# When modulation pieces are issued and reduced in the gate layer, an eviction ahead of a split, and attention heads in groups

## The chip, the cores and the metric

The kernel runs on one NeuronCore of a Trainium2 chip. The metric is the device time of one execution in microseconds (us), lower is better. TensorE (PE) multiplies, VectorE (DVE) and ScalarE (ACT) do elementwise work, GpSimd (POOL) helps them, and SyncE (SP) issues nearly all DMAs that bring weights from HBM.

## What is computed

Two transformer parts on one sequence of 256 tokens of width 1024, everything in float32. The first is a block with three kinds of attention and a gated feed-forward layer with a convolution. The second has two layers, each modulated by a condition vector. Cut to what matters here:

```
for layer in range(2):
    shift_m, scale_m, gate_m, shift_f, scale_f, gate_f = ada_mod(c, ada_w[layer], ada_b[layer])
    h = modulate(rms_norm(x, norm_gains[layer, 0]), shift_m, scale_m)
    y = attn_hybrid_mixer(...) if layer % 2 == 0 else retention_mixer(...)
    x = x + gate_m * y
    h = modulate(rms_norm(x, norm_gains[layer, 1]), shift_f, scale_f)
    x = x + gate_f * swiglu(h, w_gate_up[layer], w_down[layer])
return rms_norm(x, final_norm)
```

`ada_mod` is `silu(c) @ w + b` with a matrix of 1024 x 6144 per layer. `attn_hybrid_mixer` has eight "stick" heads (stick-breaking attention) and eight "moba" heads (softmax attention), on projections `qkv` (1024 to 3072), and an output projection (1024 to 1024). `swiglu` is `(silu(gate) * up) @ w_down` with 2816 hidden features.

## The kernel before

**Weights and chunks.** The work is a chain of phases, each a matrix product with its weights cut into chunks: `w_in`, `w_out`, `up`, `down`, `qkv` (12 chunks), `att_o` (4), `gu0` (22, the gate and up weights of layer 0), `dn0` (16, the down weights), `ret_in` (24), `ret_o`, `gu1`, `dn1`. A chunk is 16 tiles of 128x128 (1 MB), or 11 tiles in the down phases (0.7 MB). SP loads chunk n into the ring `raw0` to `raw3` (L582) when the chunk four before has been split. For float32 accuracy each weight is split in two rounded parts: ScalarE writes `w_hi` (L725, `hi(chunk)`), then VectorE `w_lo = raw - w_hi` (L2009, `lo(chunk)`), each in two halves, into two slots. A slot is free when TensorE has finished the chunk two before. TensorE then does three matmuls for each tile (L1330, L1331, L1332: hi x hi, lo x hi, hi x lo), so 48 for a full chunk and 33 for a down chunk. Results go to the PSUM banks `lin[0]` and `lin[1]` in turn; a bank must be evicted (`lin_free`) before the second next chunk starts in it.

**Modulation pieces.** The product with `ada_w` isn't done on TensorE. It comes in 48 pieces of 1 MB; SP loads a piece into one of two slots (L572, `load_ada`), and VectorE reduces it (L2093, two passes, then L2096 adds the bias; `piece`). `load_ada` waits until the piece two before has been reduced (`ada_out`), since it overwrites its slot, and everything that SP issues afterwards stands behind that wait. `ADA_STEPS` says at which step c of a phase a piece stands. Both SP and VectorE walk the phases in that order: SP issues a chunk's weights and then the step's piece; VectorE in step c splits chunk c+1 (`lo`), multiplies (`product`) or evicts, and then reduces the step's piece. The loops are unrolled by four; `steps(eng, n, lead, tail, body)` writes `lead` steps out first and `tail` last, and the pattern must repeat within the loop.

**Attention of layer 0.** The chunks of `qkv` and `att_o` are interleaved with the attention of heads, on TensorE in the table `HOOKS`: `{chunk: {tile number: stages}}` runs stages ahead of that tile. Stages work on pairs of heads: `stick_scores` (L1779, L1781), `stick_sums` (L1791 to L1793), `rotate_heads` (L1801), `moba_scores` (L1838, L1840), `moba_turn` (transposes, L1849), and `stick_values` and `moba_values` (L1813, L1815). These are plain float32 matmuls. The results of the value stages go to two banks in turn; ScalarE rounds them (`round_pair`, L1071), VectorE takes the remainder (`pair_to_split`, L2383, counted by `o_tiles`), and the next but one pair's values wait for that. The first two chunks of `att_o` are done in two parts each (`out_part`), tiles 0 to 3 and 4 to 7. VectorE evicts an `att_o` chunk with L2346 (`out(step)`), which adds it to `x`. Chunks 8 to 11 of `qkv` are wide rows (L1395 to L1398, 512 columns, 0.24 us each).

Of the kernel before, what the change touches and what calls it, by code (L numbers as in the profile page):

```python
# [110 lines left out]
def phase_of(chunk):  # L111
    for ph in ORDER:
        if chunk < ph.chunk0 + ph.n:
# [8 lines left out]
             ("gu0", 22, lambda c: int(4 <= c <= 20 and (c % 2 or c in (4, 18, 20)))), ("dn0", 16, lambda c: int(c % 2 or c in (2, 12)))]  # L122
# [4 lines left out]
def ada_before(name, c):  # L127

    n = 0
    for at, steps_, f in ADA_STEPS:  # L130
        if at == name:
            return n + sum(f(i) for i in range(c))
        n += sum(f(i) for i in range(steps_))


def ada_here(name, c):
    return ADA_AT[name](c) if name in ADA_AT else 0
# [139 lines left out]
def build(nc, dram):  # L277
    ctx = ExitStack()
    with ctx:
# [279 lines left out]
        def _(sp):  # L559
# [25 lines left out]
            def phase(ph):  # L585
                load = weights_of(ph)

                def one(step):
                    load(step)
                    if ph.name == "w_in" and step.j == 1:  # L590
                        sp.dma_start(cond_silu, dram["cond"]).then_inc(cond_in, 16)
                    if ph.name == "w_in" and step.j == 2:
                        sp.dma_start(arena[:, TAB1_AT:TAB1_AT + dram["tab1"].shape[1]], dram["tab1"]).then_inc(tab1_in, 16)
                    for m in range(ada_here(ph.name, step.j)):
                        load_ada(step, lambda c, m=m: ada_before(ph.name, c) + m)

                if ph.name == "qkv":

                    for c in range(ph.n):
                        load(Step(c))  # L600
                        for m in range(ada_here(ph.name, c - 2) if c >= 2 else 0):
                            load_ada(Step(c - 2), lambda c, m=m: ada_before(ph.name, c) + m)
                else:
                    steps(sp, ph.n, *{"gu0": (6, 1), "down": (4, 1), "dn0": (4, 1)}.get(ph.name, (4, 0)), one)
# [96 lines left out]
        def _(act):  # L701
# [252 lines left out]
            ph = PH["up"]  # L954
# [207 lines left out]
            round_pair(0)  # L1162
            hi(ph.chunk0 + 12)
            round_pair(1)
# [3 lines left out]
            qkv_unit(10)  # L1168
            hi(ph.chunk0 + 13)
            qkv_unit(11)  # L1170
            round_pair(3)
# [155 lines left out]
        def _(pe):  # L1327
# [524 lines left out]
            def run(*todo):  # L1852
# [6 lines left out]
                3: {8: run((stick_scores, 0)), 12: run((stick_scores, 1))},  # L1859
                4: {6: run((stick_scores, 2)), 10: run((stick_scores, 3))},  # L1860
                5: {8: run((rotate_heads, 0))},
                6: {6: run((rotate_heads, 1)), 10: run((stick_sums, 0), (stick_sums, 1)), 13: run((stick_sums, 2), (stick_sums, 3))},
# [3 lines left out]
                10: {0: run((moba_turn, 0)), 3: run((stick_values, 0)), 5: run((stick_values, 1)), 6: run((moba_scores, 2))},  # L1866
                11: {0: run((moba_turn, 1)), 2: run((stick_values, 2)), 4: run((moba_scores, 3)), 6: run((stick_values, 3))},
# [31 lines left out]
            out_part(0, range(0, 4), {0: run((moba_turn, 2)), 5: run((moba_values, 0))})  # L1899
            out_part(1, range(0, 4), {0: run((moba_values, 1)), 4: run((moba_turn, 3)), 6: run((moba_values, 2))})  # L1900
# [86 lines left out]
        def _(dve):  # L1987
# [455 lines left out]
            pair_to_split(0)  # L2443
            score_moba(2)
            pair_to_split(1)
            lo(ph.chunk0 + 12)
            weigh_moba(2)
            pair_to_split(2)
            score_moba(3)
            pair_to_split(3)  # L2450
# [11 lines left out]
            for c in range(1, ph.n):  # L2462
                lo(ph.chunk0 + c + 1)
                out(Step(c - 1))
                if c >= 2:
                    z_rest(L0F, ph, c - 2)
# [5 lines left out]
            def swiglu(ph, base, i):  # L2472
# [20 lines left out]
                steps(dve, ph.n, 6 if ph.name == "gu0" else 4, 1, one)  # L2493
# [340 lines left out]
```

## Time and profile before

| | us |
|---|---|
| median of 3 runs (1119.17 to 1120.69) | 1119.7 |
| the profiled execution | 1118.62 |
| its span | 1116.8 |
| TensorE busy | 1068.5 |
| VectorE busy | 792.2 |
| ScalarE busy | 595.3 |

Rows of the timeline give start and duration in us, engine, line, operation, the tile written and the tiles read, shape and count; in brackets stands the idle time of the engine before the row and what ended it. `SPq` rows are DMA issues. The ends of matmuls are modelled, and two matmuls overlap, so the distance between starts is a better measure than the duration.

### The profile page before, as it was taken

Reading aid. Unit: us, or ns where it says so; the run is one execution under the profiler, and the core shown is the slowest. Engines: PE = TensorE matmul, PEld = TensorE weight load, DVE = VectorE, ACT = ScalarE, POOL = GpSimd, SP = SyncE. Lnnn points to the kernel's source line nnn. Section 1 sums busy time; section 2 is a strip of 40 time slices with the busy share of each in tenths; the row PEclk is TensorE's granted clock in tenths of the full one; section 3 lists DMA queues with packets and bytes.
Section 4 is the critical chain, followed back from the end, with each engine's and each line's share of the span. In section 5 each row is a group of like instructions: output and inputs, shape, how many; then the busy total and the mean of one; then the engine's idle time right before and its main releaser. Section 6 shows DMA issues by size and latency. Waiting matters only on the chain.

```text
span 1116.8 us, 21680 instructions
## 1 busy us (share of the span) xinstructions
PE 1068.5 (96%) x8385; PEld 1027.0 (92%) x8385; DVE 792.2 (71%) x1375; ACT 595.3 (53%) x1016; POOL 142.6 (13%) x146
## 2 busy tenths in 40 slices
PE   6988999999899999999999999899999999999998
PEld 5877999999899998789999999897899999999997
DVE  5767659999877887667877778877557757544443
ACT  6586447776344465656544434544365557444442
POOL 0000003343210000013111101210000013111010
PEclk9999989999999899999999999999999999999999
DMA  9621345675698463255674797564434544554450
GB/s 366 216 101 51 146 188 226 253 296 194 251 348 331 161 228 120 79 208 207 255 310 173 307 352 292 221 207 181 136 129 151 189 172 156 202 188 153 156 181 38
DMA packets 34399, 226.66 MB, mean 203 GB/s; under 512 B 3827, under 2 KB 4124, under 8 KB 12444
## 3 DMA queue, kind: packets, MB, share of 16 engines
q1 hardware_dynamic: 33884, 223.11, 53.3%
q0 software_dynamic: 448, 2.63, 0.6%
q8 instruction: 45, 0.74, 0.3%
q14 instruction: 22, 0.18, 0.0%
HBM read 224.66 MB, written 2.63 MB: 204 GB/s over the span
## 4 chain that ended last, share of the span: by engine, by line
PE 74%; DVE 12%; ACT 6%; DMA 4%; issue 2%; POOL 1%; SPq 0%; DVEq 0%; ACTq 0%; POOLq 0%
PE psum L1330 20%; PE psum L1331 19%; PE psum L1332 19%; DVE w_lo L2009 4%; DVE arena L2093 3%; ACT w_hi L725 2%; PE psum L1395 2%; PE psum L1398 2%; PE psum L1397 2%; PE psum L1408 1%; DMA raw<-in_down 1%; DMA raw<-in_dn 1%; PE psum L1427 1%; DMA raw<-in_qkv 1%; DVE arena L2040 1%
## 5 line engine op out<-in xcount | busy, mean ns | idle before, releaser
L2009 DVE TENSOR_TENSOR w_lo<-raw,w_hi 128x1024 fp32r<-128x1024 f32 (+1 forms) x354 | 395.9, 1141 | 214.6 <-ACT w_hi L725 207.2
L725 ACT ACTIVATE w_hi<-raw 128x1024 fp32r<-128x1024 f32 (+1 forms) x354 | 337.7, 971 | 281.4 <-PE psum L1332 188.6
L1330 PE MATMUL psum<-h_hi,w_hi 128*128 128x256 f32 (+1 forms) x1240 | 355.8, 287 | 8.7 <-DVE w_lo L2009 3.1
L1331 PE MATMUL psum<-h_lo,w_hi 128*128 128x256 f32 (+1 forms) x1240 | 349.3, 282 | 0.0
L1332 PE MATMUL psum<-h_hi,w_lo 128*128 128x256 f32 (+1 forms) x1240 | 348.0, 281 | 0.0
L1330 PE MATMUL psum<-hid_hi,w_hi 128*128 128x256 f32 (+1 forms) x1096 | 313.4, 286 | 19.3 <-DVE w_lo L2009 11.6
L1332 PE MATMUL psum<-hid_hi,w_lo 128*128 128x256 f32 (+1 forms) x1096 | 310.4, 283 | 0.0
L1331 PE MATMUL psum<-hid_lo,w_hi 128*128 128x256 f32 (+1 forms) x1096 | 310.4, 283 | 0.0
L1330 PEld LDWEIGHTS psum<-h_hi,w_hi 128*128 128x128 f32 x1240 | 233.6, 188 | 14.1 <-issue 7.8
L1331 PEld LDWEIGHTS psum<-h_lo,w_hi 128*128 128x128 f32 x1240 | 234.6, 189 | 0.7 <-issue 0.7
L1332 PEld LDWEIGHTS psum<-h_hi,w_lo 128*128 128x128 f32 x1240 | 234.7, 189 | 0.0
L1330 PEld LDWEIGHTS psum<-hid_hi,w_hi 128*128 128x128 f32 x1096 | 208.1, 190 | 23.2 <-issue 14.6
L1332 PEld LDWEIGHTS psum<-hid_hi,w_lo 128*128 128x128 f32 x1096 | 208.2, 190 | 0.0
L1331 PEld LDWEIGHTS psum<-hid_lo,w_hi 128*128 128x128 f32 x1096 | 208.1, 190 | 0.0
L2093 DVE CUSTOM_DVE_ANT_0 arena<-arena 128x1024 f32<-128x1024 f32 x96 | 123.8, 1325 | 0.0
L638 POOL TENSOR_TENSOR arena<-arena 128x256 f32<-128x256 f32 x29 | 29.9, 1031 | 482.3 <-ACT arena L1098 331.2
L989 ACT ACTIVATE hid_hi<-arena 128x256 f32 (+1 forms) x60 | 25.1, 418 | 76.8 <-DVE arena L2254 60.7
L658 POOL TENSOR_TENSOR hid_lo<-arena,hid_hi 128x256 f32 (+1 forms) x44 | 35.4, 804 | 182.3 <-ACT hid_hi L989 174.1
L648 POOL TENSOR_TENSOR arena<-arena 128x256 f32<-128x256 f32 x22 | 31.4, 1429 | 85.8 <-ACT arena L978 85.8
L1408 PE MATMUL psum<-busy 128*128 128x256 f32 x221 | 39.2, 337 | 2.5 <-ACT busy L764 2.5
L1408 PEld LDWEIGHTS psum<-busy 128*128 128x128 f32 x221 | 35.2, 238 | 3.0 <-ACT busy L764 2.5
L2244 DVE SCALAR_TENSOR_TENSOR arena<-psum,cols,arena 128x255 f32<-128x255 f32 (+1 forms) x88 | 36.3, 473 | 1.7 <-ACT arena L968 1.0
(245 smaller groups left out, 1021.1 us busy)
## 6 DMA issues: line engine op xcount, KB each, us to landing
arena<-in_ada SPq DMA_DIRECT2D x48, 1024.0 KB, 4.9
raw<-in_gu SPq DMA_DIRECT2D x44, 1024.0 KB, 4.9
raw<-in_ret_in SPq DMA_DIRECT2D x24, 1024.0 KB, 4.8
raw<-in_up SPq DMA_DIRECT2D x22, 1024.0 KB, 7.0
raw<-in_dn SPq DMA_DIRECT2D x32, 704.0 KB, 5.9
raw<-in_qkv SPq DMA_DIRECT2D x12, 1024.0 KB, 7.7
raw<-in_down SPq DMA_DIRECT2D x16, 704.0 KB, 7.4
raw<-in_ret_o SPq DMA_DIRECT2D x8, 1024.0 KB, 4.7
```

Of the source, the lines that this page charges most:

```text
L638: nc.gpsimd.tensor_tensor(acc, acc, sq[:, k * S:(k + 1) * S], ALU.add).then_inc(sq_added, 1)
L648: nc.gpsimd.tensor_tensor(hid, ff["u"][:, 2 * at + S:2 * at + 2 * S], ff["g"][:, at:at + S], ALU.mult)\
L658: nc.gpsimd.tensor_tensor(hid_lo[:, cut], ff["hid"][:, S * (j % 2):S * (j % 2) + S], hid_hi[:, cut].bitcast(F32), ALU.subtract).then_inc(h ...
L725: nc.scalar.activation(w_hi[chunk % SPLIT_SLOTS][:, a:b], raw[chunk % RAW_SLOTS][:, a:b], ACT.Copy)\
L989: nc.scalar.activation(hid_hi[:, bass.ds(step.n(lambda c: (c - lag) * S), S)], ff["hid"][:, S * (j % 2):S * (j % 2) + S], ACT.Copy).then_i ...
L1330: nc.tensor.matmul(out, w[0], hc, start=start, stop=False, skip_group_check=True)
L1331: nc.tensor.matmul(out, w[0], lc, start=False, stop=False, skip_group_check=True)
L1332: return nc.tensor.matmul(out, w[1], hc, start=False, stop=stop, skip_group_check=True)
L1408: nc.tensor.matmul(bank[:, 0:S], busy[:, 0:P], busy[:, :], start=True, stop=True)
L2009: tt(w_lo[s][:, a:b], raw[chunk % RAW_SLOTS][:, a:b], w_hi[s][:, a:b].bitcast(F32), ALU.subtract)\
L2093: ins = nc.vector.tensor_tensor_reduce(w, w, cond_silu, 1.0, 0.0, ALU.mult, ALU.add, sums[:, b:b + 1])
L2244: ins = stt(u[:, back:S], bank[:, S * s:S * s + S - back], w, u[:, back:S], ALU.mult, ALU.add)
```

## The change

It does three things.

1. `gu0` has pieces at steps 4 to 9, 11, 13, 15 and 17 to 20 (13 instead of 11), `dn0` at the odd steps (8 instead of 10). In `gu0`, SP issues the piece of step c behind the weights of chunk c+2; the last ones follow behind chunk 21.
2. In `att_o`, VectorE evicts chunk 0 ahead of the split of chunk 2, not after it.
3. Stages of heads are moved so that they stand next to each other on TensorE, and ScalarE and VectorE take pairs 0 and 1, and 2 and 3, together.

```diff
-             ("gu0", 22, lambda c: int(4 <= c <= 20 and (c % 2 or c in (4, 18, 20)))), ("dn0", 16, lambda c: int(c % 2 or c in (2, 12)))]
+             ("gu0", 22, lambda c: int(4 <= c <= 20 and (c % 2 or c in (4, 6, 8, 18, 20)))), ("dn0", 16, lambda c: c % 2)]
...
-                    for m in range(ada_here(ph.name, step.j)):
-                        load_ada(step, lambda c, m=m: ada_before(ph.name, c) + m)
+                    late = 2 if ph.name == "gu0" else 0
+                    for m in range(ada_here(ph.name, step.j - late) if step.j >= late else 0):
+                        load_ada(step, lambda c, m=m: ada_before(ph.name, c - late) + m)
...
-                    steps(sp, ph.n, *{"gu0": (6, 1), "down": (4, 1), "dn0": (4, 1)}.get(ph.name, (4, 0)), one)
+                    steps(sp, ph.n, *{"gu0": (12, 1), "down": (4, 1)}.get(ph.name, (4, 0)), one)
+                    for c in (20, 21) if ph.name == "gu0" else ():
+                        for m in range(ada_here(ph.name, c)):
+                            load_ada(Step(c), lambda c, m=m: ada_before(ph.name, c) + m)
...
             round_pair(0)
+            round_pair(1)
             hi(ph.chunk0 + 12)
-            round_pair(1)
...
             qkv_unit(10)
+            round_pair(3)
             hi(ph.chunk0 + 13)
             qkv_unit(11)
-            round_pair(3)
...
-                3: {8: run((stick_scores, 0)), 12: run((stick_scores, 1))},
-                4: {6: run((stick_scores, 2)), 10: run((stick_scores, 3))},
+                3: {11: run((stick_scores, 0), (stick_scores, 1))},
+                4: {9: run((stick_scores, 2), (stick_scores, 3))},
...
-                6: {6: run((rotate_heads, 1)), 10: run((stick_sums, 0), (stick_sums, 1)), 13: run((stick_sums, 2), (stick_sums, 3))},
+                6: {8: run((rotate_heads, 1)), 10: run((stick_sums, 0), (stick_sums, 1)), 13: run((stick_sums, 2), (stick_sums, 3))},
...
-                10: {0: run((moba_turn, 0)), 3: run((stick_values, 0)), 5: run((stick_values, 1)), 6: run((moba_scores, 2))},
-                11: {0: run((moba_turn, 1)), 2: run((stick_values, 2)), 4: run((moba_scores, 3)), 6: run((stick_values, 3))},
+                10: {0: run((moba_turn, 0)), 4: run((stick_values, 0), (stick_values, 1), (moba_scores, 2))},
+                11: {0: run((moba_turn, 1)), 4: run((stick_values, 2), (stick_values, 3), (moba_scores, 3))},
...
-            out_part(0, range(0, 4), {0: run((moba_turn, 2)), 5: run((moba_values, 0))})
-            out_part(1, range(0, 4), {0: run((moba_values, 1)), 4: run((moba_turn, 3)), 6: run((moba_values, 2))})
+            out_part(0, range(0, 4), {0: run((moba_turn, 2)), 6: run((moba_values, 0), (moba_values, 1))})
+            out_part(1, range(0, 4), {1: run((moba_turn, 3))})
+            moba_values(2)
             moba_values(3)
...
             pair_to_split(0)
+            pair_to_split(1)
             score_moba(2)
-            pair_to_split(1)
...
             pair_to_split(2)
+            pair_to_split(3)
             score_moba(3)
-            pair_to_split(3)
...
+                if c == 1:
+                    out(Step(0))
                 lo(ph.chunk0 + c + 1)
-                out(Step(c - 1))
+                if c > 1:
+                    out(Step(c - 1))
...
-                steps(dve, ph.n, 6 if ph.name == "gu0" else 4, 1, one)
+                steps(dve, ph.n, 10 if ph.name == "gu0" else 4, 1, one)
```

How rows move. On SP, where `gu0` ends and `dn0` begins (`in_gu` and `in_dn` are weights, `in_ada` a piece), before:

```order
L582 DMA raw<-in_gu 128x2048
L572 DMA arena<-in_ada 128x2048
L582 DMA raw<-in_gu 128x2048
L582 DMA raw<-in_dn 128x1408 x2
L572 DMA arena<-in_ada 128x2048
L582 DMA raw<-in_dn 128x1408
L572 DMA arena<-in_ada 128x2048
L582 DMA raw<-in_dn 128x1408
L572 DMA arena<-in_ada 128x2048
```

and after:

```order
L582 DMA raw<-in_gu 128x2048
L572 DMA arena<-in_ada 128x2048 x2
L582 DMA raw<-in_dn 128x1408 x2
L572 DMA arena<-in_ada 128x2048
L582 DMA raw<-in_dn 128x1408 x2
L572 DMA arena<-in_ada 128x2048
```

Chunks 2 and 3 of `dn0` now have one piece ahead of them and none between, and two pieces of `gu0` stand ahead of chunk 0.

On VectorE, at the start of `att_o` (`w_lo` is the split, `x<-psum` the eviction), before:

```order
L2296 TENSOR_TENSOR hid_lo<-mod,hid_hi 128x8x2
L2009 TENSOR_TENSOR w_lo<-raw,w_hi 128x1024 x2
L2346 SCALAR_TENSOR_TENSOR x<-psum,mod,x 128x256 x2
L2009 TENSOR_TENSOR w_lo<-raw,w_hi 128x1024 x2
L2346 SCALAR_TENSOR_TENSOR x<-psum,mod,x 128x256 x2
```

and after:

```order
L2301 TENSOR_TENSOR hid_lo<-mod,hid_hi 128x8x2
L2351 SCALAR_TENSOR_TENSOR x<-psum,mod,x 128x256 x2
L2014 TENSOR_TENSOR w_lo<-raw,w_hi 128x1024 x4
L2351 SCALAR_TENSOR_TENSOR x<-psum,mod,x 128x256 x2
```

The first eviction stands ahead of the splits of chunks 2 and 3.

On TensorE, in the second half of `qkv` chunk 10 (64x256 are values, `arena 128x256` scores, 128x512 weights), before:

```order
L1398 MATMUL psum<-w_hi,h_lo 128x512
L1813 MATMUL psum<-arena 64x256 x2
L1815 MATMUL psum<-arena 64x128 x2
L1395 MATMUL psum<-w_hi,h_hi 128x512
L1397 MATMUL psum<-w_lo,h_hi 128x512
L1398 MATMUL psum<-w_hi,h_lo 128x512
L1838 MATMUL psum<-arena 128x256 x2
L1840 MATMUL psum<-arena 128x128 x2
L1395 MATMUL psum<-w_hi,h_hi 128x512
```

and after:

```order
L1398 MATMUL psum<-w_hi,h_lo 128x512
L1817 MATMUL psum<-arena 64x256 x2
L1819 MATMUL psum<-arena 64x128 x2
L1817 MATMUL psum<-arena 64x256 x2
L1819 MATMUL psum<-arena 64x128 x2
L1842 MATMUL psum<-arena 128x256 x2
L1844 MATMUL psum<-arena 128x128 x2
L1395 MATMUL psum<-w_hi,h_hi 128x512
```

Three stages stand together where weight matmuls stood between them.

## Rows read from the trace of the kernel before

**Rows 1.** The page: span, and TensorE's busy time.
```profile
span 1116.8 us, 21680 instructions
PE 1068.5 (96%) x8385; PEld 1027.0 (92%) x8385; DVE 792.2 (71%) x1375; ACT 595.3 (53%) x1016; POOL 142.6 (13%) x146
```

**Rows 2.** Timeline of TensorE, starts with idle time, `att_o`, `dn0`, `ret_in`.
```profile
491.37 0.36 PE L1330 MATMUL psum<-hid_hi,w_hi 128*128 128x256 f32 x1 [1.28 <-DVE x L2346]
...
649.94 0.29 PE L1332 MATMUL psum<-hid_hi,w_lo 128*128 128x256 f32 x1
652.48 0.38 PE L1330 MATMUL psum<-hid_hi,w_hi 128*128 128x256 f32 x1 [2.25 <-DVE w_lo L2009]
...
694.87 0.38 PE L1330 MATMUL psum<-hid_hi,w_hi 128*128 128x256 f32 x1 [1.46 <-DVE w_lo L2009]
...
699.29 0.38 PE L1330 MATMUL psum<-hid_hi,w_hi 128*128 128x256 f32 x1 [0.24 <-DVE w_lo L2009]
...
704.89 0.36 PE L1330 MATMUL psum<-h_hi,w_hi 128*128 128x258 f32 x1 [1.42 <-issue]
...
705.97 0.39 PE L1330 MATMUL psum<-h_hi,w_hi 128*128 128x258 f32 x1 [0.49 <-DVE w_lo L2009]
```

**Rows 3.** Stretches: us, busy of PE, PEld, DVE, ACT, POOL, clock, DMA, GB/s.
```profile
532.00:628.00 96.00, 96.00 (x802) 96.00 (x801) 75.59 (x101) 45.45 (x68) 15.07 (x17) 1.00 0.68 271
654.00:656.00 2.00, 2.00 (x12) 2.00 (x11) 1.94 (x6) 0.32 (x2) 0.00 (x0) 0.50 0.98 404
660.00:690.00 30.00, 30.00 (x255) 30.00 (x254) 26.52 (x45) 13.94 (x22) 4.74 (x4) 1.00 0.75 284
695.00:697.00 2.00, 2.00 (x18) 2.00 (x19) 2.00 (x4) 1.82 (x4) 0.10 (x1) 1.00 1.07 451
```

**Rows 4.** Timeline of SP in `dn0`: pieces (L572) and weights (L582) issued.
```profile
642.49 0.33 SPq L572 DMA_DIRECT2D arena<-in_ada  x1
643.17 0.95 SPq L582 DMA_DIRECT2D raw<-in_dn  x2
...
685.96 0.33 SPq L572 DMA_DIRECT2D arena<-in_ada  x1
686.65 0.81 SPq L582 DMA_DIRECT2D raw<-in_dn  x2
```

**Rows 5.** Timelines of VectorE and ScalarE in `dn0`: end of a piece, splits.
```profile
642.30 0.16 DVE L2096 TENSOR_TENSOR mod<-ada_sums,cols 128x2 f32<-128x2 f32 x1
...
703.57 2.35 DVE L2009 TENSOR_TENSOR w_lo<-raw,w_hi 128x1024 fp32r<-128x1024 f32 x2
...
650.51 1.47 ACT L725 ACTIVATE w_hi<-raw 128x768 fp32r<-128x768 f32 x2 [7.43 <-DMA raw<-in_dn]
...
692.91 1.47 ACT L725 ACTIVATE w_hi<-raw 128x768 fp32r<-128x768 f32 x2 [5.84 <-DMA raw<-in_dn]
```

**Rows 6.** Timeline of VectorE in `att_o`: split of chunk 2, eviction of chunk 0.
```profile
488.08 2.36 DVE L2009 TENSOR_TENSOR w_lo<-raw,w_hi 128x1024 fp32r<-128x1024 f32 x2 [2.39 <-ACT w_hi L725]
490.36 0.87 DVE L2346 SCALAR_TENSOR_TENSOR x<-psum,mod,x 128x256 f32<-128x256 f32 x2
```

**Rows 7.** Timeline of TensorE around stages of heads in `qkv` and `att_o`.
```profile
401.09 0.39 PE L1330 MATMUL psum<-h_hi,w_hi 128*128 128x256 f32 x1
...
402.71 0.70 PE L1779 MATMUL psum<-arena 64*128 64x256 f32 x4
...
422.17 1.13 PE L1801 MATMUL psum<-arena 128*128 128x512 f32 x2 [0.42 <-ACT arena L1050]
...
477.84 0.65 PE L1813 MATMUL psum<-arena 128*64 128x256 f32 x4 [0.27 <-DVE w_lo L2009]
```

**Rows 8.** Timeline of VectorE in `gu0`: splits of two steps in a row.
```profile
538.74 2.35 DVE L2009 TENSOR_TENSOR w_lo<-raw,w_hi 128x1024 fp32r<-128x1024 f32 x2
...
544.48 2.36 DVE L2009 TENSOR_TENSOR w_lo<-raw,w_hi 128x1024 fp32r<-128x1024 f32 x2
```

**Rows 9.** DMA view of the weights `in_gu` (1 MB each).
```profile
DMA to landing us min/median/max: 4.6/4.9/10.4
```

## The prediction

> **What bounds the kernel.** The profile's page first: TensorE is the engine to beat, and its own time changes only where it stops [rows 1]. So I read TensorE's timeline for starts with idle time in brackets, from `qkv` to the start of `ret_in`, the only stretch the diff touches [rows 2]; then, for each stop, the queue that fed it (SP), the engines between (ScalarE makes `w_hi`, VectorE `w_lo`), and the clock around it. Five stops lie in `dn0` and at its end, 2.25, 1.46, 0.24, 1.42 and 0.49 us, together 5.86; one lies in `att_o`, 1.28 [rows 2]. The `gu0` layer between shows none over 0.2 us.
>
> Two things make a stop dearer than its bracket. First, matmul ends are modelled: the last start before the longest stop is at 649.94, the next at 652.48, 2.54 us apart where 0.12 is normal (802 matmuls in 96 us, [rows 3]), and the first matmul after a stop takes 0.1 more; it costs 2.52 against 2.25 listed, 0.27 more [rows 2]. Second, the clock: after that stop the granted clock is 0.50, the 1.2 GHz level, and 12 matmuls fit in 2 us where 18 do in another stretch at 1.00 [rows 3]. In the timeline 16 matmuls stand that far apart (3.4 us), 0.095 more than normal each, so 1.5 us. After the 1.46 stop, in 695 to 697, the clock is 1.00 [rows 3].
>
> **Part 1, the pieces, by queue.** Why does the longest stop exist? ScalarE waits 7.43 us for the raw weights of `dn0` chunk 4 [rows 5]. Their DMA was issued at 643.17, behind a modulation piece issued at 642.49 [rows 4], and that piece waits until VectorE has finished the piece two before it, which ended at 642.46 [rows 5]. The ring slot had been free since VectorE split `dn0` chunk 0, about ten us before. So the weights are late by queue order, not by need. The same at the end: chunk 14's weights left at 686.65 behind a piece at 685.96, and ScalarE waited 5.84 us [rows 4, 5].
> After the change `dn0` has pieces at odd steps only (10 become 8, `gu0` has 13 instead of 11). The piece of step 2 no longer stands ahead of chunk 3: chunk 4 is queued behind the piece of step 3, which now waits for the one of `gu0` step 20 (done in step 20, about 628) and not for the one of `dn0` step 1. Chunk 4 can go when chunk 0 is split, about 631, 12 us earlier, against a wait of 7.43. Chunk 14 then waits for the piece of step 9 and not 11, two `dn0` chunks (7.8 us) earlier, against 5.84. Both waits go. VectorE also loses two pieces of 2.5 us there (a piece is two passes of 1.2), so its step 13 starts earlier, the piece of step 15 ends some 2 us before the last chunk does, and the split of `ret_in` chunk 0, which today starts at 703.57 [rows 5] and is what TensorE waits for at 704.89 and 705.97, is ready. What is late next is VectorE: in 660 to 690, where pieces come at odd steps only, as in the whole layer afterwards, it is busy 26.5 of 30 us, and TensorE has no stop there [rows 3]. Sum: brackets 5.86, plus 5 x 0.27 = 1.35, plus clock 1.5, makes 8.7; I keep 0.2 for a second half of `ret_in` chunk 0 that may come late. **Gain 8.5**, bounds 5 (only the two DMA waits, 4.0 with the clock and 1.0 more) and 8.9.
>
> **Part 1, what it adds.** `gu0` steps 4 to 9 now each hold a piece, six in a row. The chunk takes 48 x 0.12 = 5.76 us [rows 3], and VectorE's step with a piece 544.48 - 538.74 = 5.74 us [rows 8]. It does not fall behind, but it does not catch up either. In the step that starts at 538.74 its product ends at 541.4 (split 2.3, product 0.4) and frees a bank that TensorE wants at about 541.9 (counted back by chunks from 649.94): half a microsecond of slack. Steps 17 to 20 are such a row already and TensorE ran through them with 0.2 us of gaps. Cost 0.2; bounds 0 (and a gain of 0.2, since the weights of `gu0` chunk 20 and 21 no longer stand behind pieces) and 3 (six steps of 0.2 beyond the slack, then one spell of low clock, 1.5). DMA: a piece and a chunk are 2.1 MB per 5.76 us, 364 GB/s; the engines moved 451 in a busy stretch [rows 3]. A piece is issued when the one two before is done, and used a step and a split (2.4) later, some 8.1 us on.
> The Trainium skill (DMA: Bandwidth & Descriptors, Bandwidth) gives about 358 GB/s as the HBM limit of one core, its share when the neighbouring core streams too. By it each of these six steps would last 5.86 us, and the sum would be 0.6 us worse; the 451 GB/s of this trace speaks against it [rows 3].
>
> **Part 2, the first output chunk.** `att_o` chunk 2 needs the bank of chunk 0. Today VectorE first splits chunk 2 from 488.08 (waiting 2.39 us for `w_hi`), then evicts chunk 0 at 490.36, and TensorE starts at 491.37 [rows 2, 6]. The eviction is 0.87 us and fits into the 2.39 us in which VectorE idles; the split does not move. TensorE then starts when chunk 1 is done, and the first half of chunk 2 is split at 489.3, before that. **Gain 1.28 + 0.27 = 1.5**; bound below 1.0, if the semaphores take back some.
>
> **Part 3, heads grouped.** The switch from rounded weights to the plain float32 head matmuls costs time: between two groups of head scores stand 12 weight matmuls, which took 402.71 less the end of the group before, 401.09, so 1.62 us where 12 x 0.118 = 1.42 is normal: 0.20 for one separate stretch [rows 7]. In the wide rows, read in the same way, it was about 0.15, next to `att_o`'s values 0.18. Grouping takes away two such stretches in chunks 3 and 4 (0.40), four in 10 and 11 (0.60), two in `att_o` (0.36): 1.36. The rotation moved from block 6 to 8 of chunk 6 hides the 0.42 us wait for ScalarE's eviction [rows 7], since two blocks are 0.7 us. And `w_lo` of `att_o` chunk 1, for which 0.27 was waited at 477.84 [rows 7], comes earlier: VectorE's split of it stood behind the remainder of pair 3, whose rounding ScalarE did only after chunk 13's weights; now that rounding comes first. 1.36 + 0.42 + 0.27, and 0.05 for the modelled ends: **gain 2.1**. Below: the last turn, now at block 1 instead of 4, needs probabilities ready about 0.2 us before it, so it could wait; bounds 0 and 2.6.
>
> **Sum.** 8.5 - 0.2 + 1.5 + 2.1 = 11.9 us. The profiled execution took 1118.62 us with a span of 1116.8, so after it about 1106.7 and a span of 1104.9; the median lies 1.1 above the profiled one, so 1119.7 - 11.9 = **1107.8 us**. All of it lies on TensorE's path: nothing later has slack from the clock's side, since `ret_in`, `gu1` and `dn1` follow TensorE.
>
> **The rivals.** (a) `dn0` is bound by DMA, not queue order: it moves weights and pieces at 415 to 451 GB/s near its end [rows 3]. Then only the transfer time of two pieces goes, 2 x 2.6 = 5.2 us, and the time is 1107.8 + 3.3 = 1111.1. Against it: the burst at the end comes right after a queue was released, and in 660 to 690, at the coming density, it moves 284 GB/s at full clock [rows 3]. (b) `gu0` crowding: VectorE is late by 0.2 us a step beyond the slack and the clock falls once, +2.8, 1110.6. For it: 5.74 against 5.76. (c) A grouped hook waits: three of the new groups wait for a bank or for probabilities, one weight block of a wide row each (3 x 0.24 = 0.7), 1109.9. (d) **Slower than before**: pieces in `gu0` land late. It decides where landing takes over 8.1 us from issue; since a piece is issued only when the one two before is done, lateness doesn't shrink. At the 10.4 us that one load of this size took, four pieces are each 2.3 late, and each such stop costs the clock 1.5: 15.2 us lost, 1123.0. Against it: the median landing is 4.9 us [rows 9]. (e) The change doesn't do what it says: another wait holds chunk 4, only the end of `dn0` and parts 2 and 3 gain, 4.2 us less than said, 1112.0.
>
> **Chances.** Forecast 0.60 (own range 1106.0 to 1109.5), (a) 0.09, (b) 0.11, (c) 0.08, (d) 0.04, (e) 0.05, and 0.03 for no change within 0.2% (2.2 us), about what a measurement here can tell from none. The range holds the forecast, (a), (b), (c) and (e) up to 1112.5; below, full bounds of all parts give 1105.5. Faster by over 0.2% 0.93, same 0.03, slower 0.04.
>
> **What would show it.** TensorE's timeline has no stop over 0.3 us between `dn0`'s first chunk and `ret_in` (right) or still one near 1.5 to 2.3 after four chunks (e); the granted clock is 1.00 all through `dn0`; ScalarE's two long waits for `raw<-in_dn` are gone; `att_o` chunk 2 starts without a bracket; in `gu0` VectorE's steps 4 to 9 show no wait for `in_ada` (else d), and TensorE's brackets there sum to under 0.5 us (else b). The forecast is wrong if a piece in `gu0` makes a stop longer than about 2 us.

## The result, and the profile after

| | before | changed |
|---|---|---|
| median, runs on one chip | 1120.2 (1119.17 to 1126.35) | 1108.0 (1106.85 to 1113.06) |
| the profiled execution | 1118.62 | 1108.74 |
| its span | 1116.8 | 1106.9 |
| TensorE's idle brackets, summed | 42.2 | 35.4 |

Forecast 1107.8 us, measured 1107.99: 0.9888 of the time before, 95% interval 0.9841 to 0.9936. On another chip, in six runs of it, 1108.53 against 1121.27 (0.9881, 0.9861 to 0.9902). The total is right, but its parts were not all right, as the place-by-place reading shows.

The page of the changed kernel, against [rows 1]:

```profile
span 1106.9 us, 21659 instructions
PE 1065.8 (96%) x8385; PEld 1027.9 (93%) x8385; DVE 792.3 (72%) x1375; ACT 596.0 (54%) x1016; POOL 142.3 (13%) x146
```

TensorE's timeline from `qkv` to the start of `ret_in`, against [rows 2]. These are all its starts with more than 0.2 us of idle time from 384 to 712 us:

```profile
515.94 0.36 PE L1334 MATMUL psum<-hid_hi,w_hi 128*128 128x258 f32 x1 [1.12 <-DVE w_lo L2014]
522.66 0.39 PE L1334 MATMUL psum<-h_hi,w_hi 128*128 128x256 f32 x1 [0.72 <-ACT arena L1112]
528.79 0.38 PE L1334 MATMUL psum<-h_hi,w_hi 128*128 128x256 f32 x1 [0.21 <-DVE w_lo L2014]
710.04 0.36 PE L1334 MATMUL psum<-h_hi,w_hi 128*128 128x258 f32 x1 [1.09 <-DVE w_lo L2014]
```

What is missing here matters. The 1.28 ahead of `att_o` chunk 2 is gone, so are 0.42 and 0.27 in the attention, and the five stops of `dn0` and the start of `ret_in`. What remains stands around the start of `gu0` and in the norm of `ret_in`, which the change doesn't touch; in the kernel before, 1.12 and 0.72 stood in the first chunks of `gu0` too, so the sentence of the prediction that this layer shows none over 0.2 us misses its start. The stretches of `gu0` and `dn0`, against [rows 3] (us, busy of PE, PEld, DVE, ACT, POOL, granted clock, DMA share, GB/s), show TensorE busy throughout, at the 2.4 GHz level:

```profile
530.50:626.50 96.00, 96.00 (x802) 96.00 (x802) 83.88 (x114) 46.17 (x70) 16.68 (x18) 1.00 0.79 304
626.50:692.00 65.50, 65.50 (x548) 65.50 (x548) 52.47 (x90) 30.05 (x48) 6.90 (x7) 1.00 0.79 307
```

**Place by place.** Wherever an instruction of ScalarE stands in both kernels, the difference of its starts tells how far the program has moved by then, whatever stopped where. I took four such marks: one early in `qkv` (393.84 us in the kernel before), one in `gu0` (535.94), one in `ret_in` (713.03), one near the end (1099.65). This table is computed from the timelines of all profiled executions, each against the one profile of the kernel before. The first column is the shift at the first mark, the others what each stretch adds. Negative is earlier.

| profile | up to `qkv` | `qkv` + `att_o` | `gu0` + `dn0` | the rest |
|---|---|---|---|---|
| changed kernel | +3.46 | -4.94 | -8.35 | -0.01 |
| the same again (e9_after) | +0.17 | -4.91 | -8.34 | +2.53 |
| e1_pieces | +3.24 | +0.01 | -10.94 | +2.51 |
| e2_evict | +2.25 | -1.52 | +0.38 | +2.53 |
| e3_heads | +0.21 | -3.54 | -0.55 | +2.54 |
| e4_queue | +5.21 | +0.06 | -6.52 | +2.53 |
| e5_step2 | +3.10 | -5.05 | -7.66 | +2.55 |
| e6_order | +2.84 | -5.08 | -0.91 | +2.55 |
| e7_down | -3.58 | -4.93 | -10.94 | +2.52 |
| e8_groups | +4.85 | -5.09 | -8.34 | +2.53 |
| e10_down | -3.03 | -4.89 | -8.36 | -0.01 |
| e11_table | +4.14 | -4.87 | -0.70 | 0.00 |
| e12_crowd | +1.34 | -4.90 | -10.95 | +2.52 |

The first and the last column move although all of these kernels but e7_down and e10_down are equal to the kernel before in those stretches. The last section says why. The two middle columns are what the change does: 4.94 + 8.35 = 13.3 us in the profile, against 11.9 forecast. Of it, 3.5 us were given back ahead of `qkv` in this one execution. How much one profile can tell of a stretch is seen in `gu0` + `dn0` of e2_evict and e3_heads, whose edits lie elsewhere: +0.38 and -0.55.

### The profile page after: what moved, and what is told of

It is laid out like the page before. It is cut to its first block, busy times and chain, and to the rows that moved or that the text cites. A ratio compares the mean times of both kernels' runs of the same rounds, so it can differ in the third digit from the quotient of the medians.

```text
span 1106.9 us, 21659 instructions
## 1 busy us (share of the span) xinstructions
PE 1065.8 (96%) x8385; PEld 1027.9 (93%) x8385; DVE 792.3 (72%) x1375; ACT 596.0 (54%) x1016; POOL 142.3 (13%) x146
## 4 chain that ended last, share of the span: by engine, by line
PE 77%; DVE 9%; ACT 5%; DMA 5%; issue 2%; POOL 1%; SPq 0%; DVEq 0%; ACTq 0%; POOLq 0%
PE psum L1334 21%; PE psum L1336 20%; PE psum L1335 20%; DVE w_lo L2014 3%; DMA raw<-in_down 2%; PE psum L1399 2%; PE psum L1402 2%; PE psum L1401 2%; PE psum L1412 2%; DVE arena L2098 2%; ACT w_hi L729 2%; PE psum L1431 1%; POOL arena L682 1%; DMA raw<-in_qkv 1%; DMA raw<-in_up 1%
```

## The experiments

### One part at a time

e1_pieces is the kernel before with the changes to `ADA_STEPS`, to SyncE's issue and to the loops of `gu0` and nothing else:

```diff
-             ("gu0", 22, lambda c: int(4 <= c <= 20 and (c % 2 or c in (4, 18, 20)))), ("dn0", 16, lambda c: int(c % 2 or c in (2, 12)))]
+             ("gu0", 22, lambda c: int(4 <= c <= 20 and (c % 2 or c in (4, 6, 8, 18, 20)))), ("dn0", 16, lambda c: c % 2)]
...
+                    late = 2 if ph.name == "gu0" else 0
```

> The kernel before with part 1 alone: the new piece table and gu0's pieces issued two steps late. My theory (queue order): no stop over 0.3 us in dn0 and at ret_in, gu0 unchanged, 8.3 us faster than before (about 0.9926 of its time). Rival (DMA-bound dn0): the waits for raw<-in_dn shrink by the two pieces' transfer only, 5 us faster, with a stop near 1.5 us left. Rival (gu0 crowding): stops of 1 us or more in gu0 and under 6 us gained.

Measured: 1114.02 against 1123.32 us, 0.9913 (0.9887 to 0.9939). TensorE has no stop over 0.3 us from `gu0`'s first two (1.12 and 0.72, as before) to the norm of `ret_in`. The stretch gained 10.94 us, 2.6 more than in the changed kernel, because its matmuls stood closer: 1.7 us of it throughout `gu0`, the rest in `dn0` (last section). The rivals' stops, of 1 us or more, don't exist.

e2_evict has only the eviction ahead of the split:

```diff
+                if c == 1:
+                    out(Step(0))
                 lo(ph.chunk0 + c + 1)
-                out(Step(c - 1))
+                if c > 1:
+                    out(Step(c - 1))
```

> The kernel before with part 2 alone: att_o chunk 0 evicted ahead of the split of chunk 2. My theory: the 1.28 us bracket ahead of att_o chunk 2 goes and everything behind it starts 1.5 us earlier (0.9987). Rival: TensorE then waits for w_lo of chunk 2 instead, 0 to 0.5 us gained.

Measured: 1.52 us earlier behind `att_o` in the trace, the bracket of 1.28 gone. The time, 1123.84 against 1123.32 (1.0012, 0.9983 to 1.0041), can't show 1.5 us. Here only the trace decides.

e3_heads has only the grouped heads, on TensorE, ScalarE and VectorE:

```diff
-                3: {8: run((stick_scores, 0)), 12: run((stick_scores, 1))},
+                3: {11: run((stick_scores, 0), (stick_scores, 1))},
...
```

> The kernel before with part 3 alone: stages of heads grouped. My recorded forecast: 2.1 us gained, 0.17 for each of eight merges, the rest waits. New theory from comparing the two traces: 3.3 us, because each merge also shortens the stages themselves (two value stages alone 0.80 us each, merged 1.45 together), so 0.3 per merge. Rival: the larger gain of the trace belongs to the combination with parts 1 and 2; then this run shows 2.1 or less.

Measured: 1119.05 against 1123.32, 0.9972 (0.9948 to 0.9997); in the trace 3.54 us earlier behind `att_o`. With part 2's 1.52 this makes 5.06, and the whole change gained 4.94 there: the parts add up, and the larger gain isn't their interplay. Where it comes from is seen in the rows of the stages themselves. In the kernel before, two value stages and the scores behind them in `qkv` chunk 10:

```profile
457.19 0.65 PE L1813 MATMUL psum<-arena 128*64 128x256 f32 x4
457.67 0.39 PE L1815 MATMUL psum<-arena 128*64 128x128 f32 x4
457.99 0.50 PE L1395 MATMUL psum<-w_hi,h_hi 128*128 128x512 f32 x1
...
459.58 0.65 PE L1813 MATMUL psum<-arena 128*64 128x256 f32 x4
460.06 0.39 PE L1815 MATMUL psum<-arena 128*64 128x128 f32 x4
460.38 0.50 PE L1395 MATMUL psum<-w_hi,h_hi 128*128 128x512 f32 x1
...
461.28 0.70 PE L1838 MATMUL psum<-arena 64*128 64x256 f32 x4
```

and the same in e3_heads:

```profile
456.61 0.65 PE L1813 MATMUL psum<-arena 128*64 128x256 f32 x4
457.09 0.39 PE L1815 MATMUL psum<-arena 128*64 128x128 f32 x4
457.31 0.60 PE L1813 MATMUL psum<-arena 128*64 128x256 f32 x4
457.74 0.39 PE L1815 MATMUL psum<-arena 128*64 128x128 f32 x4
458.06 0.70 PE L1838 MATMUL psum<-arena 64*128 64x256 f32 x4
```

By starts, a value stage alone takes 457.99 - 457.19 = 0.80 us, and two make 1.60. Together they take 458.06 - 456.61 = 1.45: the four matmuls of L1815 take 0.32 ahead of weight matmuls and 0.22 ahead of a second value stage, whose L1813 then takes 0.43 and not 0.48. Ahead of the scores (L1838) they take 0.32 again, so a merge of values with scores saves nothing inside the stages. A merge of two like stages saves on both sides: 0.15 in these stages, and some 0.2 in the weight matmuls around these (an estimate: 1.15 us for the four merges of chunks 10 and 11, less 0.15 for each of the two of values with values, over four). The prediction had counted only the weight matmuls, at 0.15.

### Is it every merge?

e8_groups merges two more places of the changed kernel:

```diff
-                6: {8: run((rotate_heads, 1)), 10: run((stick_sums, 0), (stick_sums, 1)), 13: run((stick_sums, 2), (stick_sums, 3))},
+                6: {8: run((rotate_heads, 1)), 13: run((stick_sums, 0), (stick_sums, 1), (stick_sums, 2), (stick_sums, 3))},
...
-                8: {4: run((rotate_heads, 3)), 6: run((moba_scores, 0))},
+                8: {6: run((rotate_heads, 3), (moba_scores, 0))},
```

> The changed kernel with two more merges: all four stick_sums groups of chunk 6 at tile 13 (before tiles 10 and 13), and in chunk 8 the last rotation moved from tile 4 to 6, next to moba_scores of pair 0. Theory (0.3 us per merge, in the stages and in the weight matmuls around them): TensorE 0.4 to 0.7 us earlier at the end of qkv. Rival (the gain of grouping was bound to the value stages and the waits): 0 to 0.2 us.

Measured: 1109.74 against 1122.91 (0.9881, 0.9831 to 0.9930). Against the profile of the changed kernel the shift is 1.22 us ahead of these places and 1.20 behind them: 0.02 gained. The rival holds, and my price of 0.3 per merge was too general. What tells the stages apart in the rows is the shape. The merges that paid are those among scores and values, whose matmuls are 64*128 or 128*64; the sums and rotations are 128*128, like the weights around them, and putting them next to each other, or a rotation next to scores, saved nothing. That shape is the cause is a reading of these rows; no run changed the shape alone.

### Queue order or bandwidth?

e4_queue keeps everything of the kernel before, its ten pieces in `dn0` too, and lets SyncE issue them two steps later:

```diff
+                    late = 2 if ph.name == "dn0" else 0
+                    for m in range(ada_here(ph.name, step.j - late) if step.j >= late else 0):
+                        load_ada(step, lambda c, m=m: ada_before(ph.name, c - late) + m)
```

> The kernel before with its own piece table (dn0 has ten pieces, same bytes, same VectorE work); only the order in which SyncE issues dn0 changes: each piece two steps later, behind the weights of chunk c+2. Queue theory: ScalarE's waits of 7.43 and 5.84 us for raw<-in_dn go, and with them the stops of 2.25 and 1.46 us and the low clock; 5.5 to 8 us faster, what is left are stops for VectorE at the end. Bandwidth theory: the bytes are the same, so the waits stay, 0 to 1 us. VectorE theory (it is the pieces' work in steps 1 to 3 that is late): 0 to 1 us too, but with ScalarE's waits gone and stops ended by w_lo while VectorE has no idle time ahead of them.

Measured: 1119.14 against 1123.32, 0.9958 (0.9935 to 0.9980), and 6.5 us earlier at `ret_in` in the trace. The medians differ by 4.2 us only; their interval, 2.2 to 7.3, holds the 6.5. ScalarE's waits of 7.43 and 5.84 us [rows 5] are gone, with the bytes unchanged; its longest wait for a chunk of `dn0` is now one for TensorE:

```profile
646.07 0.85 ACT L729 ACTIVATE w_hi<-raw 128x768 fp32r<-128x768 f32 x1 [1.46 <-PE psum L1336]
```

The granted clock stays at 1.00 where it was 0.50 [rows 3]:

```profile
654.00:656.00 2.00, 2.00 (x19) 2.00 (x18) 2.00 (x4) 1.07 (x2) 0.00 (x0) 1.00 1.04 408
```

So the stops came from what stood ahead of the weights in the queue. What is left of them is VectorE's, which still has ten pieces there and splits `ret_in` chunk 0 late:

```profile
703.11 0.36 PE L1334 MATMUL psum<-h_hi,w_hi 128*128 128x258 f32 x1 [0.53 <-issue]
704.73 0.39 PE L1334 MATMUL psum<-h_hi,w_hi 128*128 128x258 f32 x1 [1.03 <-DVE w_lo L2013]
```

VectorE has no idle time from 690 us to this split, which starts at 701.79. That is the rest up to the 8.35 us: the order of the queue is worth 6.5 us, and by difference the two pieces taken from VectorE 1.8, each give or take the 0.5 by which profiles of equal code differ in this stretch.

e11_table is the opposite: the changed kernel, late issue kept, with the piece table of before.

```diff
-             ("gu0", 22, lambda c: int(4 <= c <= 20 and (c % 2 or c in (4, 6, 8, 18, 20)))), ("dn0", 16, lambda c: c % 2)]
+             ("gu0", 22, lambda c: int(4 <= c <= 20 and (c % 2 or c in (4, 18, 20)))), ("dn0", 16, lambda c: int(c % 2 or c in (2, 12)))]
```

> The changed kernel with the piece table of before (gu0 11 pieces, dn0 10), the late issue in gu0 kept: only the table is undone. If queue order in dn0 is the cause, both stops return, ahead of chunk 4 and at chunk 14, and ret_in waits again. Their size tells what set it: 2.25 us with the low clock behind it, as before (weights landing 7.3 us after their issue), would give 8 us more than the changed kernel at the start of ret_in; 0.7 us without it, as in the run with step 2 alone (landing 5.8 us), would give 4 to 5 us.

Measured: 1116.76 us, beside 1108.53 of the changed kernel: 8.2 more, and 7.65 more in the trace. All five stops are back. The first is the same as before, low clock included (0.57 is between the two levels, a mean over the stretch):

```profile
651.45 0.58 PE L1334 MATMUL psum<-hid_hi,w_hi 128*128 128x256 f32 x1 [2.15 <-DVE w_lo L2014]
```
```profile
651.00:655.00 4.00, 3.55 (x17) 3.55 (x18) 3.93 (x8) 2.18 (x4) 0.00 (x0) 0.57 0.99 408
```

So the late issue in `gu0` does nothing for `dn0`; the table does, and e6_order below, with the table and without the late issue, has no stop in `dn0`.

e5_step2 puts one piece back:

```diff
-             ("gu0", 22, lambda c: int(4 <= c <= 20 and (c % 2 or c in (4, 6, 8, 18, 20)))), ("dn0", 16, lambda c: c % 2)]
+             ("gu0", 22, lambda c: int(4 <= c <= 20 and (c % 2 or c in (4, 8, 18, 20)))), ("dn0", 16, lambda c: int(c % 2 or c == 2))]
```

> The changed kernel with one piece back in dn0 step 2 (gu0 step 6 gives it up); all else as changed. Queue theory: piece 3 again waits for the piece of step 1, chunk 4's weights stand behind it, and the stop ahead of dn0 chunk 4 returns with the low clock behind it: a stop of about 2.25 us, 2.52 + 1.5 = 4.0 us later at the end of dn0 than the changed kernel, and nothing at chunk 14. Rival (bandwidth: the sum of bytes in dn0 decides): one piece more of 2.6 us transfer, half a stop at each end, 0 to 1.5 us. Rival (the clock term isn't real): 2.5 us.

Measured: 1111.55 us (0.9903, 0.9866 to 0.9941, of the kernel before on that chip). The stop stands where the queue theory puts it, and only there, but it is small. Timelines of TensorE, SyncE and ScalarE:

```profile
648.80 0.38 PE L1334 MATMUL psum<-hid_hi,w_hi 128*128 128x256 f32 x1 [0.71 <-DVE w_lo L2014]
```
```profile
640.36 0.33 SPq L572 DMA_DIRECT2D arena<-in_ada  x1
641.04 0.95 SPq L582 DMA_DIRECT2D raw<-in_dn  x2
```
```profile
646.83 1.47 ACT L729 ACTIVATE w_hi<-raw 128x768 fp32r<-128x768 f32 x2 [5.88 <-DMA raw<-in_dn]
```

The order in the queue is that of before, and the weights leave equally late. But ScalarE can start 646.83 - 641.04 = 5.8 us after the issue, where it took 650.51 - 643.17 = 7.3 us [rows 4, 5] in the kernel before, and 7.2 in e11_table. The difference, 1.5 us, is the difference of the stops (2.25 and 0.71). The granted clock behind the small stop is 1.00. So I was right on the place and wrong on the price: 4.0 expected, 0.7 found. The load behind it had no such gain: ScalarE could start on chunk 5 only after another wait,

```profile
649.88 0.85 ACT L729 ACTIVATE w_hi<-raw 128x768 fp32r<-128x768 f32 x1 [1.58 <-DMA raw<-in_dn]
```

9.5 us after the piece ahead of both was issued (640.36), and in the kernel before it was 652.14 - 642.49 = 9.65. So the three loads took about as long together, and chunk 4's finished earlier within them. Why is open: e5_step2 has nine pieces in `dn0`, so the piece ahead of chunk 4 goes to the other slot, and no run took these two apart.

### What lets gu0 carry six in a row

e6_order is the changed kernel with its table, and the issue as before:

```diff
-                    late = 2 if ph.name == "gu0" else 0
-                    for m in range(ada_here(ph.name, step.j - late) if step.j >= late else 0):
-                        load_ada(step, lambda c, m=m: ada_before(ph.name, c - late) + m)
+                    for m in range(ada_here(ph.name, step.j)):
+                        load_ada(step, lambda c, m=m: ada_before(ph.name, c) + m)
```

> The changed kernel without the late issue in gu0: same piece table, but SyncE issues each piece behind its own step's weights, as in the kernel before. My theory: six pieces in a row put weights of chunk c+1 behind a piece that waits for step c-2, so the weights leave about two steps (11.5 us) ahead of their use against a landing of about 5 us: ScalarE's waits for raw<-in_gu appear, but no stop of TensorE over 0.3 us in gu0; under 1 us lost. Rival: as in dn0, the weights are late by queue order and stops of 1 to 2.5 us appear in gu0, 3 us or more lost.

Measured: 1115.33 us (0.9937, 0.9919 to 0.9955), beside 1109.74 and 1111.55 of e8_groups and e5_step2 on the same chip. My theory fell. TensorE, then SyncE and ScalarE:

```profile
547.77 0.39 PE L1330 MATMUL psum<-h_hi,w_hi 128*128 128x256 f32 x1 [2.22 <-DVE arena L2255]
...
562.77 0.39 PE L1330 MATMUL psum<-h_hi,w_hi 128*128 128x256 f32 x1 [3.21 <-DVE arena L2255]
```
```profile
536.60 0.33 SPq L572 DMA_DIRECT2D arena<-in_ada  x1
536.97 0.43 SPq L582 DMA_DIRECT2D raw<-in_gu  x1
```
```profile
543.93 2.01 ACT L725 ACTIVATE w_hi<-raw 128x1024 fp32r<-128x1024 f32 x2 [4.20 <-DMA raw<-in_gu]
```

I had reckoned with a landing of 5 us, the median of [rows 9]. A load that is issued right behind another one shares the queue with it: here ScalarE started 543.93 - 536.97 = 7.0 us after the issue. Each of the two stops costs its bracket and 0.27, the second also 1.5 us of clock (1.00 behind the first, 0.50 behind the second). The stretch gained 0.91 us in place of 8.35, so the late issue is worth 7.4 us. The table alone would have moved the stops from `dn0` into `gu0`.

e12_crowd goes on: eight in a row in `gu0` (steps 4 to 11), seven pieces left in `dn0`.

> The changed kernel with one piece more in gu0 (step 10, so eight in a row, steps 4 to 11) and one less in dn0 (step 15); loops of gu0 written out. VectorE needs 5.74 us for a step with a piece, TensorE 5.72 to 5.76 us for a chunk at the common spacing and 5.60 at the tight one. Theory: at the common spacing VectorE just keeps up, no stop, same time as the changed kernel within 1 us. Rival (the slack of 0.5 us is used up after six steps): stops from step 9 on, 1 to 3 us lost.

Measured: 1107.95 us (0.9897, 0.9866 to 0.9929), beside 1108.53 of the changed kernel on that chip: the same. No new stop over 0.3 us in `gu0` or `dn0`. VectorE's split starts, in the row of eight, against [rows 8]:

```profile
540.79 2.36 DVE L2014 TENSOR_TENSOR w_lo<-raw,w_hi 128x1024 fp32r<-128x1024 f32 x2
546.42 2.35 DVE L2014 TENSOR_TENSOR w_lo<-raw,w_hi 128x1024 fp32r<-128x1024 f32 x2
552.04 2.35 DVE L2014 TENSOR_TENSOR w_lo<-raw,w_hi 128x1024 fp32r<-128x1024 f32 x2
```

A step with a piece takes VectorE 5.62 us in a row of such steps, not the 5.74 that I had read off [rows 8]. In this profile the matmuls stood close, a chunk in 5.60 us, so VectorE lost 0.02 us a step and eight steps made no stop; at the common spacing (5.71) it gains on TensorE. So `gu0` takes at least one piece more, and there was nothing to win by taking it out of `dn0`: 10.95 us in the stretch, beside the 10.94 of e1_pieces and e7_down at the same close spacing.

### A version that beats both

The first `down` layer has the same pattern: four pieces in steps 0 to 3 and weights behind them. The changed kernel's TensorE (e9_after; in the first profile the same places show 2.53, 1.46 and 0.21):

```profile
304.77 0.39 PE L1334 MATMUL psum<-hid_hi,w_hi 128*128 128x256 f32 x1 [2.57 <-DVE w_lo L2014]
310.75 0.38 PE L1334 MATMUL psum<-hid_hi,w_hi 128*128 128x256 f32 x1 [1.80 <-DVE w_lo L2014]
315.45 0.39 PE L1334 MATMUL psum<-hid_hi,w_hi 128*128 128x256 f32 x1 [0.53 <-DVE w_lo L2014]
```

```diff
-                    late = 2 if ph.name == "gu0" else 0
+                    late = 2 if ph.name in ("gu0", "down") else 0
...
-                    steps(sp, ph.n, *{"gu0": (12, 1), "down": (4, 1)}.get(ph.name, (4, 0)), one)
-                    for c in (20, 21) if ph.name == "gu0" else ():
+                    steps(sp, ph.n, *{"gu0": (12, 1), "down": (6, 0)}.get(ph.name, (4, 0)), one)
+                    for c in {"gu0": (20, 21), "down": (14, 15)}.get(ph.name, ()):
```

> The changed kernel with the late issue in the first down layer too (pieces two steps behind their weights; its 11 pieces stay). There stand stops of 2.53, 1.46, 0.21 and 0.93 us, with ScalarE waiting 5.29, 3.46, 4.09 and 5.18 us for raw<-in_down. Queue theory: the first three go with the clock loss behind them, 4 to 6 us faster than the changed kernel up to the start of qkv. VectorE theory: four pieces in steps 0 to 3 need 4.2 us a chunk against 4.0, so small stops ended by w_lo stay and 1 to 3 us are gained. Bandwidth theory: nothing, 0 us.

Measured: 1103.97 against 1122.91, 0.9840 (0.9805 to 0.9875). Of the four stops one of 0.56 us is left; the gain in the trace, 6.2 us, lies just above what the queue theory gave. In the changed kernel's profiles no low clock stood behind these stops, so it is the brackets that went. Was the trace a lucky one? Two more runs asked that.

> The changed kernel again, unaltered, on one chip with the next ones: a base for them. If the two kinds of difference seen between profiles (2 to 4 us ahead of qkv, and a spacing of matmuls in gu0, ret_in and gu1 that differs by 2% at a granted clock of 1.00) come from the execution and not from the code, this profile shows another mixture of them than the first one of the same kernel, while the stops in qkv, att_o, gu0 and dn0 stay as they were: none over 0.3 us but the 1.1, 0.7 and 0.2 around gu0's start.

> The changed kernel with the late issue in the first down layer too, again, in five rounds beside the changed kernel: is it faster than both? By the first trace of it 6.2 us at the start of qkv, so about 0.9945 of the changed kernel; if that trace was lucky in its first part, 4 us (0.9965).

Measured side by side: 1108.53 (0.9881) for the changed kernel and 1101.56 us (0.9819, 0.9795 to 0.9844) for this one, 7.0 us faster. The second profile of the changed kernel shows what its expectation said: -4.91 and -8.34 in the two middle columns, as in the first, and other values in the outer ones. From 276 us to the first mark in `qkv` its two profiles gain 6.2 and 6.1 us on the first profile of the changed kernel (whose second one differs from it by 0.4 there). Of the four stops one is left in e10_down, ended by VectorE's split:

```profile
314.46 0.39 PE L1334 MATMUL psum<-hid_hi,w_hi 128*128 128x256 f32 x1 [1.14 <-DVE w_lo L2014]
```

This is the fastest kernel of the study, by the part of the change that looked least like a gain.

## Why the prediction was right, point by point

- **Pieces in `dn0`, 8.5 forecast, 8.35 found.** Every step held: five brackets of 5.86 are gone, ScalarE's two long waits too, the clock is 1.00 all through `dn0`, and chunk 4 was issued as soon as its slot came free (VectorE's split of chunk 0 in the changed kernel, then SyncE):

```profile
626.82 1.77 DVE L2014 TENSOR_TENSOR w_lo<-raw,w_hi 128x768 fp32r<-128x768 f32 x2
```
```profile
628.78 0.34 SPq L582 DMA_DIRECT2D raw<-in_dn  x1
```

These two rows speak against rival (e), another wait, and e4_queue against rival (a), bandwidth; neither is left standing. (Rival (a) quotes 415 to 451 GB/s; its rows 3 show 404 and 451.) The 1.5 us of clock in the sum were there to win in the one profile that it is measured against; the profile of e2_evict lost them elsewhere (last section).
- **`gu0`'s cost, 0.2 forecast, 0.0 found.** The shift at `gu0`'s start is -1.48 and at its end -1.48. VectorE shows no wait for `in_ada` there. The slack was larger than I wrote: a step takes 5.62 us; of the 5.74 of [rows 8], 0.12 passed between the end of the piece and the next split. Rivals (b) and (d) fell.
- **What the prediction did not price: the late issue.** It stands in my sum only as a possible gain of 0.2. It is worth 7.4 us (e6_order), since without it the same table makes stops in `gu0`. I had followed the queue in `dn0`, where weights stood behind pieces, and not asked what six pieces in a row would do to the weights of `gu0` in the old order. The total did not suffer, because the change has both; as far as the forecast goes, that is luck.
- **First output chunk, 1.5 forecast, 1.52 found.**
- **Grouping, 2.1 forecast (at most 2.6), 3.4 found**: the one term that was mis-sized, beyond its bounds. By place in the changed kernel's trace: chunks 3 and 4 gained 0.65 (0.40 forecast), the moved rotation 0.69 (0.42, and the 0.27 of the modelled end beside it, which I had counted for long stops and not here), chunks 10 and 11 1.15 (0.60), `att_o` 0.92 (0.36 and 0.27). The step that failed is the price of a merge, read from the weight matmuls between two groups alone; inside the stages two like ones side by side save another 0.15 us (values) to 0.2 (two score stages take 0.86 us each alone in the kernel before, 1.50 together in e3_heads). Rival (c), a hook that waits, fell: no group has a bracket.
- **The DMA rate.** From 540 to 570 us, with a piece in nearly every step, the changed kernel moved 376 to 378 GB/s in both profiles with TensorE never idle, and the six steps were not stretched. The 358 GB/s that the Trainium skill (DMA: Bandwidth & Descriptors, Bandwidth) gives as a core's share when both cores of a pair stream therefore did not bind here; the measurement decides, and the 0.6 us by it did not come. What the neighbouring core did, no run shows.
- **The total.** 13.3 us in the two stretches against 11.9: the error is all in the grouping. It is also just past the full bounds of all parts (8.9 + 0.2 + 1.5 + 2.6 = 13.2). From the median these give 1106.5 us; the 1105.5 of the prediction takes them from the profiled execution, while its forecast starts from the median. That the median still came out within 0.2 us of the forecast is chance, since executions of one kernel differ by several us elsewhere (last section). On the second chip the gain was 12.7.

## What to carry to other kernels

When an engine waits for a load, look at what its queue was told to wait for before that load; issuing the things that must wait behind the things that must not cost nothing that the traces show and was worth 6.5 us here in one layer, 7.4 in another and 6 in a third. Price a load that is issued right behind another one by that pair's own landing time (5.8 to 7.3 us here), not by the median of loads of its kind (4.9). Compare kernels place by place, by the start of the same instruction in both traces, before believing or doubting a total.

## What the hardware showed that I had not expected

**Two spacings at one granted clock.** Windows of TensorE alone (us, busy and number of matmuls, clock, DMA share, GB/s) in `gu1`, of the kernel before and of e9_after, the same code there:

```profile
960.00:990.00 30.00, 30.00 (x257) 1.00 0.52 178
```
```profile
960.00:990.00 30.00, 30.00 (x252) 1.00 0.53 181
```

and in `gu0`, of e12_crowd and the changed kernel:

```profile
540.00:570.00 30.00, 30.00 (x257) 1.00 0.96 377
```
```profile
540.00:570.00 30.00, 30.00 (x252) 1.00 0.95 378
```

TensorE is busy all the time, the clock is granted in full, and yet 2% more or fewer matmuls fit in. It isn't the kernel: the changed kernel shows 257 in `gu1` in one profile and 252 in the other (e9_after). In the table it is the 2.5 us of the last column, which is 0 in four profiles and +2.5 in the other ten, and the 2.6 us by which e1_pieces, e7_down and e12_crowd exceed 8.35. No profile has the close spacing all through both layers. What sets it is open.

**Ahead of `qkv`, up to 5 us from one execution to the next.** In code that is the same in all, one profile of the changed kernel has a granted clock below 1.00 behind a stop of 3.26 us, and the other one has none behind the same stop:

```profile
60.00:72.00 12.00, 11.52 (x85) 0.86 0.19 68
```
```profile
60.00:72.00 12.00, 12.00 (x102) 1.00 0.28 83
```

That is 1.5 of its 3.5 us. So a stop does not always cost the clock: the clock was below 1.00 behind stops of 2.25, 2.19, 2.15 and 3.21 us (before, e3_heads, e11_table, e6_order), and 1.00 behind others of 2.22 us (e6_order), 2.53 us (the changed kernel, in `down`) and 2.29 us (e2_evict, the very stop of `dn0` that had 0.50 behind it in the kernel before). The plainest pair is one stop of `down`, 2.69 us long in both the kernel before and e3_heads, and the 3 us behind it, in this order:

```profile
305.00:308.00 3.00, 3.00 (x16) 3.00 (x16) 2.88 (x6) 0.00 (x0) 0.00 (x0) 0.50 0.97 401
```
```profile
306.00:309.00 3.00, 3.00 (x28) 3.00 (x27) 2.81 (x6) 0.00 (x0) 0.00 (x0) 1.00 1.00 410
```

The 1.5 us that I had added for the clock in `dn0` were lost there in the profiles of before, e3_heads and e11_table, and not in that of e2_evict, which gained 1.3 us at this stop and lost 1.5 at the start of `ret_in`, where its clock fell to 0.50 behind stops of 1.42 and 0.49 us that had 1.00 behind them in the kernel before. Such a term can be read from a trace, but not told from the length of a stop.
